# One block for the even mixer: latents' columns first, attention and linear attention between half units of the projection, and the odd layer's constants loaded a layer earlier

## What is computed

```
h = x @ w_in                       # 1024 -> 1984 columns
c_q, c_kv, k_pe, gq, gk, gv, g_lr, gr = split(h, (256, 128, 32, 256, 256, 512, 32, 512))
q = rms(c_q) @ w_uq ; k_nope, v = rms(c_kv) @ w_ukv ; q_pe, k_pe = rope(...)
o_mla = softmax((q_nope k_nope + q_pe k_pe) * scale) v
la = log_sigmoid(g_lr @ gate_w + gate_b) / 16                    # two directions
o_gla = rms(gla(gq, gk, gv, la_fwd) + flipped gla(la_bwd)) * silu(gr)
x = layer_norm(alpha * x + concat(o_mla, o_gla) @ w_o)
x = layer_norm(alpha * x + experts(x) + sigmoid(x @ ple_gate_w + b) * (p @ ple_w))
```

## Time and profile before

| | |
|---|---|
| median of 3 runs | 2459.01 us (2457.14 to 2460.61) |
| the profiled execution | 2458.51 us, span 2456.7 us |
| PE busy | 2085.9 us, 85% of the span |
| DVE, ACT busy | 1036.7 us (42%), 716.3 us (29%) |
| DMA | 623.81 MB, 254 GB/s in the mean |

### The profile page before, as it was taken

The page is one execution under the profiler, slowest core; times in us unless marked ns, Lnnn a source line. Parts: engine busy times, 40 slices in busy tenths (PEclk is TensorE's granted clock), DMA queues, the critical chain, the costliest instruction groups (busy, mean ns, idle before and its releaser), DMA issues. The chain is left out here.

```text
span 2456.7 us, 31051 instructions
## 1 busy us (share of the span) xinstructions
PE 2085.9 (85%) x12588; PEld 1392.5 (57%) x12588; DVE 1036.7 (42%) x1538; ACT 716.3 (29%) x995; POOL 78.8 (3%) x148
## 2 busy tenths in 40 slices
PE   8779977776777897767777999978999999978998
PEld 6455522222245653222223888766888888766886
DVE  3335200000047621000002776665776776665775
ACT  3523201000025331000002333534333333534332
POOL 0000000000002000000000000010000000010000
PEclk9769998988889999898988999988999999988999
DMA  8114999999981399999999555422555555422551
GB/s 330 58 39 179 422 426 427 426 427 426 427 322 69 133 382 426 425 426 426 426 427 359 189 185 208 146 95 81 193 172 170 188 185 208 146 95 80 192 174 42
DMA packets 192687, 623.81 MB, mean 254 GB/s; under 512 B 17542, under 2 KB 114920, under 8 KB 159848
## 3 DMA queue, kind: packets, MB, share of 16 engines
q1 hardware_dynamic: 192616, 622.84, 65.7%
HBM read 621.76 MB, written 1.05 MB: 254 GB/s over the span
## 5 line engine op out<-in xcount | busy, mean ns | idle before, releaser
L1775 PE MATMUL psum<-weight_ring,arena 128*32 128x256 f32 x4096 | 281.9, 430 | 131.8 <-DMA weight_ring<-in_w 131.8
L2321 PE MATMUL psum<-x_both,up_hi 128*128 128x512 f32 x1408 | 359.8, 397 | 3.1 <-DVE x_both L469 3.0
L1775 PEld LDWEIGHTS psum<-weight_ring,arena 128*32 128x32 f32 x4096 | 134.1, 120 | 281.4 <-DMA weight_ring<-in_w 170.6
L2321 PEld LDWEIGHTS psum<-x_both,up_hi 128*128 128x128 f32 x1408 | 258.0, 188 | 61.7 <-DVE x_both L469 4.5
L1792 PE MATMUL psum<-weight_ring,arena 128*32 128x512 f32 x1024 | 242.3, 651 | 48.2 <-DMA weight_ring<-in_w 40.4
L1875 DVE TENSOR_TENSOR arena<-arena,psum 128x256 f32<-128x256 f32 x32 | 13.5, 421 | 506.7 <-PE psum L1775 506.7
L577 PE MATMUL psum<-w_hi,x_both 128*128 128x512 f32 (+2 forms) x800 | 210.0, 390 | 13.6 <-DVE mix_lo L709 10.1
L2369 DVE TENSOR_TENSOR up_lo<-weight_ring,up_hi 128x2048 fp32r<-128x2048 f32 x88 | 201.3, 2291 | 19.2 <-ACT up_hi L2343 18.9
L2324 PEld LDWEIGHTS psum<-x_both,up_lo 128*128 128x128 f32 x1408 | 192.2, 188 | 15.5
L2324 PE MATMUL psum<-x_both,up_lo 128*128 128x256 f32 x1408 | 197.0, 282 | 0.0
L2381 DVE TENSOR_REDUCE arena<-psum 128x256 f32<-128x512 f32 x176 | 113.3, 686 | 186.9 <-PE psum L2324 186.9
(11 more groups left out here) (322 smaller groups left out, 2339.5 us busy)
## 6 DMA issues: line engine op xcount, KB each, us to landing
weight_ring<-in_w SPq DMA_DIRECT2D x192, 2048.0 KB, 25.7
weight_ring<-in_ffn_wg SPq DMA_DIRECT2D x44, 1024.0 KB, 5.5
weight_ring<-in_ffn_wu SPq DMA_DIRECT2D x44, 1024.0 KB, 8.0
weight_ring<-in_ffn_wd SPq DMA_DIRECT2D x44, 1024.0 KB, 5.0
weight_ring<-in_w_in SPq DMA_DIRECT2D x12, 2048.0 KB, 8.2
weight_ring<-in_w_o SPq DMA_DIRECT2D x4, 2048.0 KB, 19.8
weight_ring<-in_ple_gate_w SPq DMA_DIRECT2D x4, 2048.0 KB, 10.9
weight_ring<-in_w_out SPq DMA_DIRECT2D x4, 2048.0 KB, 8.0
```

What stands on the lines that cost most here:

```text
L1775: last = pe.matmul(ps[j * CAP:(j + 1) * CAP, 4 + k // 2, 0:QW], tokens_now[:, cc, :], w[:, c, j * QW:(j + 1) * QW], start=cc == 0, stop=cc ...
L2321: last = pe.matmul(ps[:, 4 + 2 * f + h, :], w_part[:, f, h, c, :], x_both[:, :, c, :], start=c == 0, stop=False, skip_group_check=True)
```

## The change

The blocks of the even mixer become one, `even_mixer`, in which each engine's order is written out. The projection's columns are read in another order and in other widths, and four ring units become blanks: no load, their slots serve as scratch (attention's columns, probabilities, decay factors, states). `mix_out_norm` gets its job begun, with half a unit of `w_o` done. In the linear attention the masked scores of both directions are added on DVE before they are multiplied. The odd layer's gains, positions and frequencies get places of their own and are loaded in layer 0's `experts`.

```diff
+EVEN_UNITS = [(0, O_GQ), (O_LR, (EVEN_IN - O_LR) // 2), (O_LR + (EVEN_IN - O_LR) // 2, (EVEN_IN - O_LR) // 2),
+              (O_GQ, 2 * GLA_HEADS * DK), (O_GV, GLA_HEADS * DV)]
+EVEN_BLANKS = 4
...
-            matrix(t["w_in_even"][0], EVEN_IN)
+            matrix(t["w_in_even"][0], EVEN_IN, units=EVEN_UNITS)
             stream.add(up_projections, 0, 2)
+            for _ in range(EVEN_BLANKS):
+                stream.add(lambda slot, _: [], 0, 0)
...
     def mix_out_norm(block, layer, attended=None, begun=None):
...
-            job.products(pe, 0)
+            job.products(pe, 0, None if begun is None else 1)
             params_ready(pe)
...
+            if begun is not None:
+                part_mix(dve, 1)
+                for k in range(1, 4):
+                    job.part_low(dve, k // 2, k % 2)
...
+    def even_mixer(block):
...
+        def load(sp):
+            stream.issue(sp, first + 2)
+            load_params(sp, (norm_cols[:, 0:2], t["mla_q_norm"][0].rearrange("(c p) -> p c", p=P)),
...
+            load_constants(sp)
+            sp.wait_ge(cleared.sem, cleared.at(1))
+            load_params(sp, (gate_w[0:RANK, 0:width], t["gla_gate_w_fwd"][0]),
...
+            stream.issue(sp, blanks[-1] + 1)
...
+        def norm_rows(sp):
+            sp.wait_ge(cums.sem, cums.at(3))
+            load_params(sp, (ln_params[:, 0, :], spread(t["ln1_g"][0])), (ln_params[:, 1, :], spread(t["ln1_b"][0])))
...
+        def mask_scores(dve, d):
...
+            if d == 1:
+                dve.wait_ge(masked.sem, masked.at(4))
+                for hh in range(2):
+                    dve.tensor_tensor(att[:, hh], att[:, hh], att_back[:, hh], ALU.add).then_inc(masked.sem, 1)
...
+        @block.tensor
+        def _(pe):
+            half = lambda n: job.products(pe, n // 2, n % 2)
+            half(0), half(1), half(2)
+            turn_latents(pe)
+            half(3)
+            up_products(pe, 0)
+            half(4)
+            turn_gate_inputs(pe)
+            up_products(pe, 1)
+            logit_products(pe)
+            half(5)
+            pe.wait_ge(logits_taken.sem, logits_taken.at(1))
+            half(6)
+            turn_heads(pe)
+            sum_decays(pe)
+            half(7)
+            score(pe, 0)
+            pe.wait_ge(exps.sem, exps.at(2))
+            half(8)
+            turn_gla(pe)
+            score(pe, 1)
+            turn(pe, 0)
+            half(9)
+            score(pe, 2)
+            turn(pe, 1)
+            sum_values(pe, 0)
+            chunk_scores(pe, 0)
+            score(pe, 3)
+            turn(pe, 2)
+            sum_values(pe, 1)
+            chunk_scores(pe, 1)
+            turn(pe, 3)
+            sum_values(pe, 2)
+            update_products(pe)
+            sum_values(pe, 3)
+            chunk_products(pe, 0), chunk_products(pe, 1)
+            out_job.products(pe, 0, 0)
+            turn_outputs(pe, 0), turn_outputs(pe, 1)
...
+        @block.vector
...
+            store(dve, 0)
+            mask_scores(dve, 0)
+            normalise(dve, 4), normalise(dve, 5)
+            peaks(dve, 6), peaks(dve, 7)
+            store(dve, 1)
+            mask_scores(dve, 1)
+            normalise(dve, 6), normalise(dve, 7)
+            store(dve, 2)
+            run_states(dve)
+            store(dve, 3)
+            dve.wait_ge(stored.sem, stored.at(MLA_HEADS // 2))
+            dve.memset(stat[:, 24:25], 0.0).then_inc(stream.used, 2)
+            part_mix(dve, 0)
+            out_job.part_low(dve, 0, 0)
+            norm_outputs(dve, 0)
+            norm_outputs(dve, 1)
...
+            dve.memset(stat[:, 24:25], 0.0).then_inc(stream.used, 2)
+            dve.wait_ge(mix_kept.sem, mix_kept.at(2))
...
+        @block.sync
+        def _(sp):
+            norm_rows(sp)
+            stream.issue(sp)
...
         def heads_on_vector(dve, k):
-            if k == 0:
-                gain_tables(dve)
             if k == 1:
                 tables.reduce_angles(dve)
+            if k == 2:
+                gain_tables(dve)
+            if k == 3:
+                sum_heads(dve, 0)
             if k == 4:
-                sum_heads(dve, 0)
+                finish_keys(dve)
+                params_ready(dve)
             if k == 5:
-                finish_keys(dve)
+                sum_heads(dve, 1)
                 rotate_heads(dve, 1).then_inc(rotated.sem, 1)
-                sum_heads(dve, 1)
...
             sp.wait_ge(mixed.sem, mixed.at(0))
+            if layer == 0:
+                load_odd_constants(sp)
...
     with nc.Block() as block:
-        h = even_projection(block)
-    base, log_decays, gla_gain = latent_attention(h)
-    gla(h, base, log_decays, gla_gain)
-    with nc.Block() as block:
-        mix_out_norm(block, 0)
+        out_job = even_mixer(block)
+        mix_out_norm(block, 0, begun=out_job)
```

More of the change, by code:

```diff
@@ new lines, in square_latents @@
+        def square_latents(act):
+            act.wait_ge(kept.sem, kept.at(TILES))
+            for a in range(TILES):
+                act.activation(q[:, a, 0:4, 0:64], h[:, a, O_CQ:O_CQ + Q_LORA].rearrange("p (u d) -> p u d", d=64),
+                               ACT.Square, accum_out=sums[:, a:a + 1]).then_inc(squared.sem, 1)
+                act.activation(q[:, a, 4:6, 0:64], h[:, a, O_CKV:O_CKV + KV_LORA].rearrange("p (u d) -> p u d", d=64),
+                               ACT.Square, accum_out=sums[:, 2 + a:3 + a]).then_inc(squared.sem, 1)
@@ L1357, in gla @@
-        scaled.advance(2), cums.advance(3), exps.advance(3)
-        for s in (turned, taken, tails, silus, ups, states, outs, squares, rooted,
-                  normed, mixed):
-            s.advance(1)
-        atts.advance(4), masked.advance(4)
+                        last = pe.matmul(ps[:, hh, (2 * pr + a) * P:(2 * pr + a + 1) * P],
+                                         shrink[half, d, pr, a * P:(a + 1) * P], q_up[half, d, pr, a * P:(a + 1) * P],
+                                         start=True, stop=True)
@@ new lines, in _, with keep @@
+        @block.scalar
+        def _(act):
+            def keep(i):
+                job.wait(act, i)
+                n0, w = EVEN_UNITS[i]
+                for a in range(TILES):
+                    bank = ps[:, (TILES * i + a) % 4, 0:w]
+                    split = max(0, min(w, O_GR - n0)) if n0 + w > O_GR else w
+                    if split:
+                        last = act.copy(h[:, a, n0:n0 + split], bank[:, 0:split])
+                    if split < w:
+                        last = act.activation(h[:, a, n0 + split:n0 + w], bank[:, split:], ACT.Silu)
+                    last.then_inc(kept.sem, 1)
+            part = lambda n: job.part_high(act, n // 2, n % 2)
+            part(2)
+            keep(0)
+            part(3)
+            square_latents(act)
+            part(4)
+            keep_latents(act)
+            keep(1)
+            part(5)
+            keep_up(act, 0)
+            part(6)
+            keep_up(act, 1)
+            keep(2)
+            part(7)
+            soften(act)
+            part(8)
+            for g in range(0, 8, 2):
+                place_heads(act.copy, act, g)
+            decay_factors(act)
+            tail_factors(act)
+            keep(3)
+            part(9)
+            exponentials(act, 0), exponentials(act, 1)
+            take_gla(act)
+            exponentials(act, 2), exponentials(act, 3)
+            keep_turned(act, 0)
+            keep(4)
+            exponentials(act, 4), exponentials(act, 5)
+            keep_turned(act, 1)
+            exponentials(act, 6), exponentials(act, 7)
+            keep_turned(act, 2), keep_turned(act, 3)
+            out_job.part_high(act, 0, 0), out_job.part_high(act, 0, 1)
+            square_outputs(act, 0), square_outputs(act, 1)
+            keep_outputs(act)
```

913 lines of the change are left out of this document (526 added, 387 removed).

## The result

The changed kernel takes **2429.47 us** (median of three runs, 2427.63 to 2429.72), the kernel before 2459.81 in the same series: a ratio of 0.9872, 95% interval 0.9851 to 0.9893. The forecast was 2432.0 in a range of 2420 to 2448. (One more execution, of 10,886 us, was disturbed and is left out.) The profiled execution took 2429.22 us, its span is 2427.4: 29.3 less than before, where the sum had 26.5.

A forecast was written before the change was run, and what follows sets the result against it. Full DMA engines bound the two expert plateaus, so time saved ahead of them passes to the end: 2458.5 less 14.5 (even layer) and 12 (odd layer) gives 2432.0 us, range 2420 to 2448.

The forecast's parts named there:

- the sum: Whole kernel: 2458.5 less 14.5 for the even layer and 12 for the odd layer gives 2432.0 us.
- Part 1: Even mixer's projection: up-projection weights land late, so up products start at 35.7 us and PE idles for 7 us.
- Part 2: Even mixer, up products to chunk products: PE work 68 us, idle start 2.5, waits 14; first chunk product at 120.
- The rival in which the braid stalls: Even mixer: some 60 hand-overs between three engines cost more than given; 2436 to 2446 us, middle 2443; chance 0.17.
- Part 3: Chunk products 12.6 us at half clock, first w_o half 8.0, second half waits 3.5 and ends at about 152.5.
- Part 4: Between w_o's units: PE idles 12.5 us for p, queued behind weights; gate term at 179.5, even layer gains 14.5.
- the rival without the wait: Between w_o's units: p arrives in time, no 12.5 us idle or half clock, 11.4 net; 2420.6 us; chance 0.05.
- The clock, weighed: Even mixer's chunk products: kept at clock 0.50 as in the earlier profile row, against the skill's rule; 12.6 us.
- Part 5: Odd layer: early constants remove 8.0 us idle and 2.7 of half clock, first peaks 1.4 sooner; 12 us gain.
- The slower rival, a late ring: First expert stage: scratch slots delay ring refill, 5.0 us per missing unit, six give 2461.8 us; chance 0.03.

The follow-up runs named there:

- the kernel with these weights first: On Early p, the up-projection weights' load issued right behind the second projection unit, ahead of thirteen small loads and units 3 to 5: 2402.51 us.
- Early p: Changed kernel with SyncE issuing the load of p ahead of the two weight units that wait for w_o's slots: 2413.58 us.
- the filled gaps: On Early p, idle products in two TensorE waits: 12 ahead of the last probabilities' transposes, 10 ahead of the chunk products: 2402.69 us.
- first gap only: On Early p, only the 12 idle products ahead of the last probabilities' transposes, the wait before the chunk products left open: 2409.83 us.
- all together: On Early p, up-projection weights issued early and idle products in both waits, before the last probabilities' transposes and the chunk products: 2394.11 us.
- odd alone: Kernel before with only the odd layer's part: constants loaded in layer 0, keys turned inside the projection, new VectorE and ScalarE order: 2441.34 us.

## Why the prediction held, point by point

- **Part 1, up weights late.** Forecast 35.7 for the first up products, measured 38.44, behind 9.94 us of idle. The mechanism is as told, and the kernel with these weights first shows it. The term that was mis-sized is the thirteen small loads: costed at 4 us, they took some 6.7 (38.4 less the 31.7 of the kernel before); their upper bound was 8.6. They also kept SP, which issued the next unit of the projection at 16.33 only. From 16 to 20 us the DMA engines were at a share of 0.47 and 124 GB/s, where the kernel before had 1.05 and 388.
- **Part 2, the braid.** Forecast 84.3 us from there to the chunk products, measured 82.5. The waits on the timeline are the ones named, not all in their sizes: 2.4 behind the head copies (4.5), 0.15 behind the normalisation (1), 3.45 behind the last probabilities (4), 2.29 for the states (2.5). That is 8.4 us of idle where the forecast had 12, with PE busy for 74.1 us where it had 72.9 (68, and 2.5 and 2.4 for the clock). So the total is closer than its terms, and its error of 1.8 takes back most of part 1's 2.7: that is luck. The rival in which the braid stalls did not come about.
- **Part 3.** Chunk products 13.0 (12.6), first `w_o` half 8.2 to 8.3 (8.0), wait 3.46 (3.5), end at 153.7 (152.5).
- **Part 4.** 13.0 us of idle for p (12.5), the first gate-term product at 180.0 (179.1). Early p shows the cause, SP's order. The price of the rival without the wait was too low: 11.4 net was written, 14.9 us at the gate term and 15.9 at the end were measured. The forecast's own terms give more than 11.4, 12.5 of idle and 2.5 for the half that starts at half clock; it took 3.6 off again and named no step for it, and none is seen. With early p, PE goes on at once, and the turns of p with `w_o`'s second unit take 11.6 us instead of 13.1.
- **The clock, weighed.** The size was right and the reason wrong, so the 12.6 us are right by luck: the new order happens to have a wait ahead of these products too. I took 0.50 as what these products get; the filled gaps show that it follows from what is ahead of them, here a wait of 2.29 us. The Trainium skill, "TensorE: Matmul & The Clock Gate", Part 1, says that recent busyness sets the ratio and that sustained work releases it. The first half of that agrees with the runs: gap filled, clock 1.00. The second half agrees for the wide products of `w_o` (half clock up to 139.4, full from there) and not for the chunk products, which were busy for the whole 12.9 us and stayed at 0.50. What the wide ones have that the small ones lack was not tried.
- **Part 5, the odd layer.** Forecast 12. The projection gave 10.8; the step that fell short is the attention: its first peaks did come 1.3 us sooner after the scores (1.4 forecast), but its last value products ran at half clock and only 0.5 of it was left, and `w_o` started slower too. In all the layer gave 11.3 us, against bounds of 8 to 13.
- **The sum.** 26.5 forecast for the moved work, 25.3 measured with the address held as before; by the profile 13.8 and 11.3. The 5.0 us of the address were in no term: I let the shift pass on to the end with everything behind the plateaus at its old length, and did not look at what a moved declaration does to addresses. The forecast landed in its range with it or without.
- **The slower rival, a late ring.** The plateau keeps its length and rate; nothing of it is seen.

## What to carry to other kernels

An in-order queue of loads must be read as a chain: a small load that stands behind big ones that wait for slots inherits their waits, and moving it gave more here than the odd layer's whole part. A short wait of TensorE can cost more than its length: price also the products behind it at half clock, and where nothing useful fits, try products whose result nobody reads. A difference of a few us between two such kernels needs its runs and not one profile each: the same wait kept the clock in one of these kernels and lost it in another. When two profiles differ in code that the change doesn't touch, compare the allocation as well as the instructions, and run the suspect line alone before any of the difference is credited to the idea.

## What the runs showed of the hardware that was not expected

- **The clock falls behind the wait, not in it.** After 2.29 us of idle up to two blocks ran at full speed, then it was 0.50 for the other six and for most of the `w_o` half behind them: 4.9 us and 2.8 us more than with both gaps filled. The same wait of 3.46 us between `w_o`'s halves was followed by full clock in some of these kernels (both gaps filled, first gap only) and by half clock for the 16 products behind it in another (all together). So a single profile doesn't say that a gap is harmless.
- **Busy at half clock isn't always a way out of it.** The update products were busy for 4.60 us, the chunk products for 11 us on end at 0.50; ten idle products of 128x512 in bf16 brought 1.00 back in 2.7 us.
- **32 bytes.** Shifting one allocation by 32 bytes makes the fp32r up products 394 instead of 397 ns and 279 instead of 282, and the kernel 5.0 to 6.7 us quicker, repeatably in both directions: the ten profiles at the new address have 16.65 or 16.66 us per unit, the four at the old one 16.83 or 16.84. The products of `w_hi` and `w_lo` with `x_both`, shifted the other way, became slower by 1.9 ns each. The Trainium skill, "SBUF — State Buffer", section "Specifications (TRN2)", has cachelines of 16 bytes and a penalty for each crossing into a new one. Both places of the arena are multiples of 32, so by that rule there is no difference; the measurement decides. Most of it goes with multiples of 64 bytes, the products of `w_o` with `mix_lo` don't, and the cause is open.
- **Part of odd alone.** Its 18.1 us are 10.5 up to layer 1's p and some 5 to 6.7 of the address; 1 to 3 are left over. Its profile and that of early p have one stretch in the second block, between the output projections' loads of its two layers, of 547.5 us; the other eight profiles at the new address, the changed kernel's with 550.4 among them, have 550.3 to 551.2. Why was not found.
